# Half projection tiles between the last prompt steps of a two-layer hybrid decoder step

## What is computed

```
for l in range(DEPTH):
    xp = xp + 0.5 * _swiglu(_rmsnorm(xp, norm_ffn1[l]), ffn1_gate[l], ffn1_up[l], ffn1_down[l])
    out_p, ... = _mix(_rmsnorm(xp, norm_mix[l]), w_in[l], ..., w_o[l], ..., attn_p)
    xp = xp + out_p
    xp = xp + 0.5 * _swiglu(_rmsnorm(xp, norm_ffn2[l]), ...)      # xs, the sample rows, go the same way

def _mix(...):
    z = h @ w_in_l
    bg, cg, xin, u, q, k, v, qi, ki, wi = jnp.split(z, pts, axis=-1)
    y_conv, y_pool = _short_conv(...), _multi_pool(...)
    y_attn = attn_fn(q, k, v, qi, wi, ki)      # index scores, top-k keys, softmax with a distance bias
    return jnp.concatenate([y_conv, y_pool, y_attn], axis=-1) @ w_o_l, ...
```

## Time and profile before

| | |
|---|---|
| median of three runs | 2418.09 us (2415.92 to 2419.88) |
| the profiled execution | 2420.59 us, span 2418.9 us, granted clock 0.982 |
| PE busy | 2323.7 us, 96% of the span |
| POOL busy | 1007.4 us, 42% |
| DVE busy | 1069.1 us, 44% |
| ACT busy | 762.1 us, 32% |
| DMA | 267.57 MB, mean 111 GB/s |

### The profile page before, as it was taken

How to read it: one execution, slowest core, us unless ns; L and a number is a source line. 1 busy time by engine, 2 the same in 40 slices (tenths; PEclk the granted TensorE clock), 3 DMA queues, 4 the chain that set the end, 5 groups by cost and what they waited for, 6 DMA issues and landing times.

```text
span 2418.9 us, 52209 instructions
## 1 busy us (share of the span) xinstructions
PE 2323.7 (96%) x19163; PEld 2212.4 (91%) x19163; DVE 1069.1 (44%) x1794; ACT 762.1 (32%) x1087; POOL 1007.4 (42%) x543
## 2 busy tenths in 40 slices
PE   6999999899988999999999999998999899999998
PEld 5999999879855999999999999997997479999998
DVE  4233233679754323323353323355895533332334
ACT  4222222543334422222242222244224443222224
POOL 4433433536515443343443443352662344344332
PEclk8999999999999999999999999999999999999999
DMA  4333322313694332332323333321248842232231
GB/s 133 115 94 111 109 87 77 83 44 88 218 306 153 106 91 75 95 95 76 99 81 105 103 109 97 96 74 53 70 120 265 295 122 75 83 95 88 77 95 63
DMA packets 335540, 267.57 MB, mean 111 GB/s; under 512 B 35438, under 2 KB 283720, under 8 KB 335392
## 3 DMA queue, kind: packets, MB, share of 16 engines
q1 hardware_dynamic: 334880, 265.73, 35.8%
q0 software_dynamic: 512, 0.13, 0.0%
q10 hardware_dynamic: 16, 0.02, 0.0%
HBM read 258.72 MB, written 12.49 MB: 112 GB/s over the span
## 4 chain that ended last, share of the span: by engine, by line
PE 90%; issue 3%; ACT 3%; DVE 2%; SPq 1%; POOL 1%; DMA 0%; DVEq 0%; ACTq 0%; POOLq 0%
PE ps L1386 81%; PE ps L1648 2%; PE ps L1669 1%; PE ps L1701 1%; PE ps L1742 1%; DVE probs L1300 1%; PE ps L1561 1%; ACT probs L828 0%; DVE normed L1091 0%; PE ps L1578 0%; PE ps L1732 0%; PE ps L1723 0%; PE ps L1660 0%; PE ps L1628 0%; ACT h_hi L628 0%
## 5 line engine op out<-in xcount | busy, mean ns | idle before, releaser
L876 POOL TENSOR_TENSOR w_lo<-raw,w_hi 128x1024 fp32r<-128x1024 f32 (+1 forms) x336 | 796.5, 2383 | 1122.7 <-ACT w_hi L615 1118.6
L1386 PE MATMUL ps<-h_hi,w_hi 128*128 128x272 f32 x3904 | 812.9, 289 | 31.0 <-POOL h_lo L881 10.6
L1386 PE MATMUL ps<-h_hi,w_lo 128*128 128x272 f32 x3904 | 808.0, 289 | 0.0
L1386 PE MATMUL ps<-h_lo,w_hi 128*128 128x272 f32 x3648 | 757.2, 289 | 0.0
L1386 PEld LDWEIGHTS ps<-h_hi,w_hi 128*128 128x128 f32 x3904 | 613.5, 190 | 35.7 <-issue 16.3
L1386 PEld LDWEIGHTS ps<-h_hi,w_lo 128*128 128x128 f32 x3904 | 614.4, 190 | 0.0
L1386 PEld LDWEIGHTS ps<-h_lo,w_hi 128*128 128x128 f32 x3648 | 574.9, 189 | 0.0
L615 ACT ACTIVATE w_hi<-raw 128x1024 fp32r<-128x1024 f32 (+1 forms) x336 | 343.0, 1042 | 217.3 <-DMA raw<-in_ffn_gate 173.0
L1127 DVE SCALAR_TENSOR_TENSOR xT<-ps,xT 128x544 f32<-128x544 f32 x352 | 254.9, 724 | 249.8 <-PE ps L1386 248.7
L1386 PE MATMUL ps<-act_hi,w_hi 128*128 128x272 f32 x1408 | 290.6, 287 | 0.0
L1386 PE MATMUL ps<-act_hi,w_lo 128*128 128x272 f32 x1408 | 289.8, 288 | 0.0
(11 more groups left out here) (231 smaller groups left out, 1742.1 us busy)
## 6 DMA issues: line engine op xcount, KB each, us to landing
raw<-in_ffn_gate SPq DMA_DIRECT2D x88, 512.0 KB, 3.7
raw<-in_ffn_up SPq DMA_DIRECT2D x88, 512.0 KB, 3.8
raw<-in_ffn_down SPq DMA_DIRECT2D x88, 512.0 KB, 3.4
ring<-in_cache_k SPq DMA_DIRECT2D x128, 256.0 KB, 3.6
ring<-in_cache_v SPq DMA_DIRECT2D x128, 256.0 KB, 3.5
raw<-in_w_in SPq DMA_DIRECT2D x48, 512.0 KB, 3.7
raw<-in_w_o SPq DMA_DIRECT2D x16, 512.0 KB, 4.5
bias_by_distance<-bias_by_distance SPq DMA_DIRECT2D x16, 317.0 KB
```

What stands on the lines that cost most here:

```text
L876: pool.tensor_tensor(w_lo[:, c % 6, 0:n], raw[:, c % 3, 0:n], w_hi[:, c % 6, 0:n].bitcast(F32), ALU.subtract).then_inc(units_split, 1)
L1386: ins = pe.matmul(out[:, hf, :], w, x[:, HT * hf:HT * (hf + 1)], start=first and w is w0 and x is xh, stop=last and w is w1)
```

## The change

It has four parts. At the start all five x tiles are loaded at once into slots of their own, the one-hots, `relx` and `vrows` move out of the weight slots, the bias tables go to other banks, and ACT and POOL no longer wait for `bias_s` before their first weight splits. The sample's mask and its one-hot rows are bf16, in buffers of their own. In `prompt_out` the key block is the outer loop and the head the inner one. And the w_o units are split earlier: units 0 to 5 during prompt steps 12 to 15 and the two rounds behind them, in the order in which the ring gives slots free (`O_SLOT`), with units 6 and 7 in slots 4 and 5, so behind WO4 and WO5. PE computes the first half (k 0 to 3) of WO0 before PT15, of WO1 before PO15 and of WO2 after the last `own_outputs`; the second halves follow as before. POOL makes the low part of unit 0 ahead of the strip of step 15. SP no longer waits for the last values between w_o units 1 and 2.

```
+O_SLOT = (0, 1, 2, 3, 4, 5, 4, 5)
+O_EARLY = 3
...
-        yst, yout = at("yst", [P, 2, D], r_cat), at("yout", [P, 4, D], r_cat)
+        yst, yout = at("yst", [P, 4, D], r_cat), at("yout", [P, 4, D], r_cat)
...
+        oh, relx, vrows = at("oh", [P, LS + NTP], r_cz), at("relx", [P, P], r_cz + 6720), at("vrows", [P, P], r_cz + 7232)
+        row_of_b = at("row_of_b", [32, 2 * P], region(512), BF16)
+        mask_s = at("mask_s", [32, LS], r_cat + 4 * TOK * 4, BF16)
...
             def x_rows(t):
-                if t >= 2:
-                    sp.wait_ge(tiles, t - 1)
...
-            x_rows(0)
-            x_rows(1)
+            for t in range(5):
+                x_rows(t)
...
                 o_unit(1)
-                values_read(2 * HALF - 1)
                 for n in range(2, 8):
...
             act.dma_start(a['scratch'][:, 0:ROWS, :], tp_sb[:, :].unsqueeze(1).to_broadcast([NH, ROWS, NTP])).then_inc(s_scr, 16)
-            act.wait_ge(zeroed, 4)
-            act.wait_ge(tiles, T_START)
...
                 def hi_o(n):
-                    c = 28 + n
                     if n < 6:
-                        act.wait_ge(sout_mm, l * 2 * HALF + HALF + (7, 7, 3, 3, 5, 5)[n])
-                        hi(l, 1, 0, c)
-                    else:
-                        hi(l, 1, 0, c, slot_free=T(l, f'WO{n - 6}'))
+                        act.wait_ge(sout_mm, l * 2 * HALF + HALF + (3, 3, 5, 5, 7, 7)[n])
+                    hi(l, 1, 0, 28 + n, slot_free=T(l, f'WO{n - 2}') if n >= 6 else None, slot=O_SLOT[n])
...
-                    if i >= STEPS:
-                        hi_o(i - STEPS)
-                for n in range(2, 8):
+                    if i >= STEPS - 4:
+                        hi_o(i - STEPS + 4)
+                for n in range(6, 8):
                     hi_o(n)
...
-                masked_strip(STEPS - 1)
-                for c in range(28, 36):
-                    if c < 34:
-                        hold(pool, "pool", sout_mm, l * 2 * HALF + HALF + (8, 8, 4, 4, 6, 6)[c - 28])
-                    lo(l, 1, 0, c)
+                for n in range(8):
+                    if n < 6:
+                        hold(pool, "pool", sout_mm, l * 2 * HALF + HALF + (4, 4, 6, 6, 8, 8)[n])
+                    lo(l, 1, 0, 28 + n, slot=O_SLOT[n])
+                    if n == 0:
+                        masked_strip(STEPS - 1)
...
-                dve.tensor_scalar(work_s[:, :], work_s[:, :], TAKEN / 2, NEG, ALU.is_gt, ALU.mult).then_inc(masks_done, 1)
+                dve.tensor_scalar(mask_s[:, :], work_s[:, :], TAKEN / 2, NEG, ALU.is_gt, ALU.mult).then_inc(masks_done, 1)
...
-            pe.wait_ge(x_updates, 3)
-            pe.matmul(ps[0:NH, 4, :], rel_sb[0:32, :], oh[0:32, LS:LS + 512], start=True, stop=True)
+            pe.wait_ge(x_updates, 4)
+            pe.matmul(ps[0:NH, 3, :], rel_sb[0:32, :], oh[0:32, LS:LS + 512], start=True, stop=True)
...
-                        pe.matmul(ps[:, bank, 0:t1 - t0], C('row_of', 32, P, P * g), work_s[:, t0:t1], start=True, stop=False)
+                        pe.matmul(ps[:, bank, 0:t1 - t0], row_of_b[:, P * g:P * (g + 1)], mask_s[:, t0:t1], start=True, stop=False)
...
-                    for e in range(2):
-                        h = 2 * (m % 4) + e
-                        for kb in range(m // 4 + 1):
+                    for kb in range(m // 4 + 1):
+                        for e in range(2):
+                            h = 2 * (m % 4) + e
...
+                def o_early(n):
+
+                    split_ready(l, 1, 0, 28 + n)
+                    if n == 0:
+                        hold(pe, "pe", cat_ready, (l + 1) * 4)
+                    if n < 2:
+                        hold(pe, "pe", plog_done, l * 48 + 3 * (STEPS - 2 + n) + 2)
+                    o_part(n, range(4))
...
+                    if i == STEPS:
+                        o_early(0)
                     if 1 <= i <= STEPS:
                         prompt_transposed(i - 1)
...
+                    if i == STEPS + 1:
+                        o_early(1)
                     if i >= 2:
                         prompt_out(i - 2)
...
                 own_outputs(1)
+                o_early(2)
```

More of the change, by code:

```diff
@@ L302, in trunk @@
         s_in, s_oh, s_scr, rows_copied = sem("start_loads"), sem("onehots_loaded"), sem("bias_scratch"), sem("bias_rows_copied")
-        s_xrow = [sem("xrow0"), sem("xrow1")]
+        s_xrow = [sem(f"xrow{t}") for t in range(5)]
         zeroed, relx_done, tp_done = sem("zeroed"), sem("relx_done"), sem("tp_done")
@@ L470, in _ @@
             sp.dma_start(oh[0:32, LS:LS + NTP], a['onehots'][:, NTD:NTD + NTP]).then_inc(s_oh, 16)
-            for t in range(2, 5):
-                x_rows(t)
             sp.dma_start(a['pool_sample'].rearrange("l b t c -> (l b) t c")[:, 0:11, :],
@@ L614, in hi @@
                 act.wait_ge(loaded[c % 3], raw_loads(l, ph, i, c))
-                act.activation(w_hi[:, c % 6, 0:n], raw[:, c % 3, 0:n], ACT.Copy).then_inc(units_hi, 1)
+                act.activation(w_hi[:, c % 6 if slot is None else slot, 0:n], raw[:, c % 3, 0:n], ACT.Copy).then_inc(units_hi, 1)
             AHEAD = 3
@@ L695, in _ @@
             act.wait_ge(tiles, 7)
-            act.activation(tp_sb[:, 0:512], ps[0:NH, 4, :], ACT.Copy, scale=1 / SCALE).then_inc(tp_done, 1)
-            act.activation(tp_sb[:, 512:NTP], ps[0:NH, 5, 0:NTP - 512], ACT.Copy, scale=1 / SCALE).then_inc(tp_done, 1)
+            act.activation(tp_sb[:, 0:512], ps[0:NH, 3, :], ACT.Copy, scale=1 / SCALE).then_inc(tp_done, 1)
+            act.activation(tp_sb[:, 512:NTP], ps[0:NH, 7, 0:NTP - 512], ACT.Copy, scale=1 / SCALE).then_inc(tp_done, 1)
             act.wait_ge(tp_done, 2)
             act.dma_start(a['scratch'][:, 0:ROWS, :], tp_sb[:, :].unsqueeze(1).to_broadcast([NH, ROWS, NTP])).then_inc(s_scr, 16)
-            act.wait_ge(zeroed, 4)
-            act.wait_ge(tiles, T_START)
             with act.Fori(0, DEPTH) as l:
@@ L872, in _, with lo @@
         def _(pool):
-            def lo(l, ph, i, c, n=1024):
+            def lo(l, ph, i, c, n=1024, slot=None):
                 hold(pool, "pool", units_hi, unit0(l, ph) + 6 * i + c + 1)
-                pool.tensor_tensor(w_lo[:, c % 6, 0:n], raw[:, c % 3, 0:n], w_hi[:, c % 6, 0:n].bitcast(F32), ALU.subtract).then_inc(units_split, 1)
+                at_slot = c % 6 if slot is None else slot
+                pool.tensor_tensor(w_lo[:, at_slot, 0:n], raw[:, c % 3, 0:n], w_hi[:, at_slot, 0:n].bitcast(F32), ALU.subtract).then_inc(units_split, 1)
             def raw_low(l, ph, c):
@@ L902, in _ @@
             pool.sem_inc(out_vn, 16)
-            pool.wait_ge(tiles, T_START)
             with pool.Fori(0, DEPTH) as l:
@@ L1164, in _ @@
             dve.wait_ge(tiles, 8)
-            dve.tensor_scalar(bias_s[:, :].rearrange("p (a b) -> p a b", a=3), ps[:, 0:3, 0:LT], 1 / SCALE, None, ALU.mult).then_inc(zeroed, 1)
+            dve.tensor_scalar(bias_s[:, :].rearrange("p (a b) -> p a b", a=3), ps[:, 4:7, 0:LT], 1 / SCALE, None, ALU.mult).then_inc(zeroed, 1)
+            dve.tensor_copy(row_of_b[:, :], C('row_of', 32)).then_inc(mask_b_done, 1)
             dve.tensor_copy(mask_b[0][:, :], C('causal')).then_inc(mask_b_done, 1)
@@ L1476, in _ @@
             pe.wait_ge(s_oh, 16 * (DT + 1))
-            pe.wait_ge(x_updates, 3)
-            pe.matmul(ps[0:NH, 4, :], rel_sb[0:32, :], oh[0:32, LS:LS + 512], start=True, stop=True)
-            pe.matmul(ps[0:NH, 5, 0:NTP - 512], rel_sb[0:32, :], oh[0:32, LS + 512:LS + NTP], start=True, stop=True).then_inc(tiles, 1)
-            pe.wait_ge(x_updates, 5)
-            pe.wait_ge(zeroed, 3)
+            pe.wait_ge(x_updates, 4)
+            pe.matmul(ps[0:NH, 3, :], rel_sb[0:32, :], oh[0:32, LS:LS + 512], start=True, stop=True)
+            pe.matmul(ps[0:NH, 7, 0:NTP - 512], rel_sb[0:32, :], oh[0:32, LS + 512:LS + NTP], start=True, stop=True).then_inc(tiles, 1)
             pe.wait_ge(relx_done, 1 + DT)
             for b in range(3):
-                ins = pe.matmul(ps[:, b, 0:LT], relx[:, :], oh[:, LT * b:LT * (b + 1)], start=True, stop=True)
+                ins = pe.matmul(ps[:, 4 + b, 0:LT], relx[:, :], oh[:, LT * b:LT * (b + 1)], start=True, stop=True)
             ins.then_inc(tiles, 1)
@@ L1744, in prompt_out, with o_part @@
                     ins.then_inc(tiles, 1)
+                def o_part(n, ks):
+                    wh, wl = (w[:, O_SLOT[n], :].rearrange("p (k n) -> p k n", k=KC) for w in (w_hi, w_lo))
+                    for k in ks:
+                        ins = product(pair(n % 4), wh[:, k, :], wl[:, k, :], h_hi[:, k, :], cat_lo[:, k, :], k == 0, k == KC - 1)
+                    return ins
+                def o_early(n):
[5 more added lines that the diff above has]
+                    o_part(n, range(4))
                 masks(0)
@@ L1783, in _ @@
                 own_outputs(1)
+                o_early(2)
                 for n in range(8):
-                    split_ready(l, 1, 0, 28 + n)
```

(5 more changed lines are left out.)

15 lines of the change are left out of this document (6 added, 9 removed).

## The result

The changed kernel takes 2423.59 us (median of 11 runs, 2420.94 to 2433.45), the kernel before 2417.72 (11 runs, 2412.95 to 2419.88). The ratio is 1.0029, interval 1.002 to 1.0038: slower by 5 to 9 us, where 2411.9 was forecast and the range ended at 2421.5. The two profiled spans differ by 2.0 us (2420.9 and 2418.9).

The account below looks back on a forecast made before the run. The prediction took PE's work plus its waits as the bound, weight products being 81% of the chain. Start -4.3, masks -4.5 and 2 x (7.4 - 6.1) made -6.2: 2411.9 from the median 2418.1, range 2404.0 to 2421.5.

Parts of the forecast that it names:

- The wait at tile 6: PE idle 5.1 before w_o tile 6, then 2.3 lost to lower clock: +7.4 us per layer, bounds 6.8 and 8.0.
- The first rival: No wait at w_o tile 6 because ACT's chain is hidden: the 14.8 go, giving 2397.1; chance 0.07.
- The tail: Last prompt steps: half w_o tiles fill PE's idle gaps (4.16), alternate heads save 1.95; -6.1 us per layer.
- I let this contention take about 1.0 again: Last prompt steps: POOL's w_lo beside DVE's normalising costs about 1.0, offsetting about 1.0 from step 12's shorter PO.
- the second rival: w_lo in prompt steps 13 to 15 lengthens the softmax, DVE's normalising near 2.1: +10.0, 2421.9; chance 0.10.
- The heads: PO in the last prompt steps: alternate heads overlap in PE's array, 0.9 for 16 products, 0.65 less each of three.
- The start: Before the first weight product: x tiles queued at once, ACT not waiting for bias_s; -4.3 us, between 2.6 and 6.2 saved.
- the late bound: At the start: small loads land at 13.4, ACT's copy of the bias products comes at 20.3, saving 2.6.
- The masks: Sample key tiles: three bf16 mask products about 0.5 for 2.54; 1.5 saved in layer 0, 3.0 in layer 1.
- The third rival: Front gains absorbed: small loads land late and loads bound the key tiles in both layers; -1.0, 2417.1; chance 0.14.

Follow-up runs that it names:

- ACT's order mended: Changed kernel with ffn2's first h chunks put ahead of ACT's splits of w_o units 6 and 7: 2407.94 us, ratio 0.9948 to the kernel before.
- both edits: Changed kernel with ffn2's first h chunks ahead of ACT's waiting splits and without DVE's negation of the row maxima: 2399.77 us, ratio 0.9915.
- The order experiment: Kernel with both edits, plus DVE's first four x copies at the start put ahead of the relx copies: 2391.73 us, ratio 0.9905.

## Why the prediction was wrong

**The wait at tile 6: right.** 5.1 idle was forecast and 4.97 measured in both layers; the six us behind it, at 0.53 and 0.76, lose 2.8 and 1.4 where I took 2.3. ACT's order mended shortens the tail by 9.4 and 6.5 (table), the forecast being 7.4 a layer. The 9.4 isn't the wait's alone: the stretch at the lower clock behind the negations is also shorter in that run. The first rival falls.

**The tail: the gain is right, the cover is not.** Halves and heads were to give 6.1 a layer. With the wait at tile 6 gone they give 1.7 (71.7 before, 70.0 with ACT's order mended). The step that failed is "I let this contention take about 1.0 again". With the negation gone as well the tail needs 66.5, so the gaps are filled nearly as forecast (65.6), and the contention over the negation costs 3.5 a layer (70.0 less 66.5). About half of that is PE's clock behind the wait for cat_lo, as the windows of layer 0 show, with ACT's order mended and with both edits:

```profile
756.90:764.90 8.00, 8.00 (x66) 4.87 (x67) 5.30 (x14) 5.95 (x14) 2.37 (x1) 0.79 0.24 71
```

```profile
754.00:762.00 8.00, 8.00 (x77) 5.82 (x74) 4.68 (x13) 6.24 (x12) 3.65 (x3) 1.00 0.39 111
```

The missing 0.9 no run pins down; in the kernel with both edits PE still waits 1.19 and 0.90 for the normalising of steps 12 and 13. In the changed kernel layer 0 is 2.9 longer than layer 1 (79.4 and 76.5); there the low clock behind the two waits loses 5.7 and 3.1.

I had priced POOL's splits on the long normalising and put the rest into the second rival, 2421.9 with a chance of 0.10. Its total is near what came, by luck, for it named the wrong instruction: in layer 0 the normalising stayed near 0.9 in steps 13 to 15 of the changed kernel, and the last strip was not late. What stood in the way was the two-element negation, which is on the chain from logits to exponential and had no row in my reading because it takes 0.17. The three ends above show that it waits for the end of POOL's split. The rule of the Trainium skill ("SBUF — State Buffer", section "SBUF: two separate sides") has the one engine block for the other's whole instruction, for the kinds of DVE instruction that it names. The three ends agree with that; going by its wording, I should have asked which of DVE's instructions comes during a split, however short.

**The heads: about two thirds of the size, nil by themselves.** PO fell by 0.47, not 0.65. On the kernel before, most of that reaches the first w_o product and is lost to PE's clock behind it. What it is worth with the half tiles behind it, no run separates.

**The start: a term mis-sized.** -4.3 was taken, -1.2 measured. The small loads came at the late bound, for which I had 2.6, and that bound left out that the bias products would be slower behind a wait: ACT copies their result at 21.28, not at 20.3, and so later than before (20.82). The order experiment shows in the trace that such a gain was to be had once the x copies don't wait for the small loads.

**The masks: right in layer 0, wrong in layer 1.** 1.6 for 1.5 in layer 0. In layer 1, I read 0.30 without a releaser as "no load is waited for" and took 3.0. By itself it was 0.2, since PE comes 2 us earlier and the loads don't; in the changed kernel the same stretch is 1.8 shorter (59.39 for 61.19). The third rival had this in both layers.

**Sum.** The forecast change of -6.2 and the measured one of +5.9 lie 12.1 apart. The two profiled executions differ by only 2.0. Their milestones, the changed kernel against the kernel before, us:

```
                                            measured   forecast
start, to the first weight product              -1.2       -4.3
from there to step 12 of layer 0                -3.3       -1.5
tail of layer 0                                 +7.7       +1.3
from there to the masks of layer 1              -4.6        0
on to step 12 of layer 1                        -1.4       -3.0
tail of layer 1                                 +4.8       +1.3
```

So start, masks of layer 1 and the two tails are 14.6 slower than forecast, and 6.4 comes back in the other two stretches: 8.2. The rest of the 12.1 is that the profiled execution of before was 2.9 above its median, and that of the changed kernel 1.0 below. The -4.6 lies in code that the change leaves alone; 3.4 of it are shown below.

## What to carry to other kernels

Where work is moved beside a chain of small steps, list every instruction of that chain, also those of 0.2 us, and ask what of another engine can hold each of them for that engine's whole instruction. Filling idle gaps of the bounding engine pays only as far as the engines that feed the fill have their own gaps there. And when a buffer's reuse is shifted later, look at what stands behind the new wait in the waiting engine's order: here the new order of ACT's two splits was worth 15 to 20 us.

## What the runs showed of the hardware that I had not expected

A split on POOL holds off DVE's `TENSOR_SCALAR` even at 128x2 (0.17 to 2.24), but not its `RECIPROCAL` on the same tile: without the negation it took 0.17 at 750.85, in the middle of a split that ran from 749.56 to 751.93.

The same wait does not always cost the same clock. Behind a wait of 2.20 for ACT near 1690 in both kernels, the ten us that follow ran at 0.83 before and at 1.00 afterwards, and the same twelve products took 5.32 and 3.63. At the change of layers there is the same difference, but there the waits for DVE are not equal (2.05 before, 1.52 afterwards). The rows, first of before, then of the changed kernel:

```profile
1690.55 5.32 PE L1578 MATMUL ps<-srelu,wsel 128*32 128x344 f32 x12 [2.20 <-ACT srelu L761]
...
1225.00:1235.00 10.00, 7.95 (x47) 7.34 (x46) 9.63 (x5) 3.95 (x5) 8.51 (x4) 0.83 0.31 92
1690.00:1700.00 10.00, 9.45 (x45) 5.84 (x46) 2.92 (x7) 2.49 (x3) 1.80 (x1) 0.83 0.00 0
```

```profile
1690.71 3.63 PE L1569 MATMUL ps<-srelu,wsel 128*32 128x344 f32 x12 [2.20 <-ACT srelu L755]
...
1228.00:1238.00 10.00, 8.48 (x64) 8.11 (x64) 9.78 (x5) 4.14 (x5) 9.11 (x4) 1.00 0.31 90
1690.20:1700.20 10.00, 9.49 (x59) 7.17 (x60) 4.49 (x8) 2.45 (x3) 2.39 (x1) 1.00 0.00 0
```

That is 1.7 us each, in code that the change leaves alone. Two profiled executions can so differ by some us, and a difference of milestones may only be given to a change inside the stretch that the change touches.
